# Gated blocks of two experts turned as one stack, down products two experts behind, in a one-core mixture-of-experts step

## What is computed

```python
def hier_moe(x, rg_w, rg_b, re_w, re_b, e_wg, e_wu, e_wd):
    pg = jax.nn.softmax((xt @ rg_w + rg_b).astype(f32), axis=-1)
    ...
    top_v, top_i = lax.top_k(pe, EXP_TOPK)
    ...
    for gi in range(N_GROUPS):
        h = jax.nn.silu(jnp.einsum('nd,edf->nef', xt, e_wg[gi])) * jnp.einsum('nd,edf->nef', xt, e_wu[gi])
        out = out + jnp.einsum('nef,efd->nd', h * comb[:, gi, :, None], e_wd[gi])
```

## Time and profile before

| what | value |
|---|---|
| time, median of 3 runs | 1253.25 us (1249.64 to 1254.41) |
| time of the profiled execution | 1249.23 us |
| its span in the profile | 1247.5 us |
| TensorE busy | 1219.0 us, 98% |
| VectorE, ScalarE busy | 593.5 us, 358.0 us |
| mean granted clock of TensorE | 0.993 |
| read from memory | 268.72 MB |

### The profile page before, as it was taken

How to read it: one execution, slowest core, us unless ns; L and a number is a source line. 1 busy time by engine, 2 the same in 40 slices (tenths; PEclk the granted TensorE clock), 3 DMA queues, 4 the chain that set the end, 5 groups by cost and what they waited for, 6 DMA issues and landing times.

```text
span 1247.5 us, 22834 instructions
## 1 busy us (share of the span) xinstructions
PE 1219.0 (98%) x9976; PEld 883.7 (71%) x9976; DVE 593.5 (48%) x942; ACT 358.0 (29%) x622; POOL 59.4 (5%) x99
## 2 busy tenths in 40 slices
PE   8999899999999999999999998999999999999997
PEld 8889888988898889999999885344444434444443
DVE  5346856544263543333334324445545545445545
ACT  6455343344224543322222321111111111111113
POOL 2100000001000100000000001000000000000000
PEclk9999999999999999999999999999999999999999
DMA  8210102302324723232223868999999999999993
GB/s 248 69 34 1 36 5 70 96 11 74 102 73 127 217 101 102 79 99 78 76 79 127 333 240 321 412 418 419 418 419 420 419 418 419 420 420 418 419 421 118
DMA packets 110206, 273.78 MB, mean 219 GB/s; under 512 B 22309, under 2 KB 69623, under 8 KB 85530
## 3 DMA queue, kind: packets, MB, share of 16 engines
q1 hardware_dynamic: 106234, 265.21, 56.1%
q0 software_dynamic: 2560, 4.73, 1.0%
q10 hardware_dynamic: 1312, 2.36, 0.5%
HBM read 268.72 MB, written 7.22 MB: 221 GB/s over the span
## 4 chain that ended last, share of the span: by engine, by line
PE 89%; DVE 8%; ACT 1%; issue 1%; DMA 0%; SPq 0%; ACTq 0%; DVEq 0%
PE bank L669 16%; PE bank L676 9%; PE bank L1523 7%; PE bank L817 7%; PE bank L1456 7%; PE bank L1458 7%; PE bank L1457 6%; PE bank L1583 2%; PE bank L1585 2%; PE bank L1584 2%; DVE yl L1106 2%; PE bank L864 2%; PE bank L1742 1%; PE bank L811 1%; PE bank L1696 1%
## 5 line engine op out<-in xcount | busy, mean ns | idle before, releaser
L669 PE MATMUL bank<-slot,xs 128*64 128x512 f32 x512 | 233.0, 599 | 0.9 <-DVE xs L1050 0.9
L670 PE MATMUL bank<-slot,xs 128*64 128x512 f32 x512 | 233.0, 599 | 0.0
L669 PEld LDWEIGHTS bank<-slot,xs 128*64 128x64 f32 x512 | 65.1, 137 | 124.6 <-issue 121.5
L1456 PE MATMUL bank<-xnh,wh 128*128 128x256 f32 (+1 forms) x448 | 133.3, 297 | 0.6 <-DVE mt L3087 0.6
L1458 PE MATMUL bank<-xnh,low 128*128 128x256 f32 (+1 forms) x448 | 132.8, 296 | 0.0
L1457 PE MATMUL bank<-xnl,wh 128*128 128x256 f32 (+1 forms) x448 | 132.8, 296 | 0.0
L1080 DVE TENSOR_TENSOR h<-h,bank 128x1024 f32<-128x1024 f32 (+1 forms) x73 | 86.4, 1215 | 88.9 <-PE bank L817 88.9
L2639 DVE TENSOR_TENSOR low<-ring,wh 128x1536 fp32r<-128x1536 f32 (+1 forms) x45 | 89.9, 2005 | 78.2 <-ACT wh L2278 71.3
L676 PE MATMUL bank<-slot,ht 128*64 128x512 f32 x512 | 116.9, 599 | 0.5 <-DVE ht L1100 0.5
L914 ACT ACTIVATE sg<-bank,csr 64x512 f32<-64x512 f32 x32 | 21.9, 684 | 270.4 <-PE bank L670 270.4
L1456 PEld LDWEIGHTS bank<-xnh,wh 128*128 128x128 f32 x448 | 85.1, 190 | 1.3 <-issue 1.2
(11 more groups left out here) (539 smaller groups left out, 2331.1 us busy)
## 6 DMA issues: line engine op xcount, KB each, us to landing
slot<-in_e_wg_dram SPq DMA_DIRECT2D x64, 1024.0 KB, 21.2
slot<-in_e_wu_dram SPq DMA_DIRECT2D x64, 1024.0 KB, 23.2
slot<-in_e_wd_dram SPq DMA_DIRECT2D x64, 1024.0 KB, 23.2
ring<-in_w_in_dram SPq DMA_DIRECT2D x13, 1024.0 KB, 5.3
ring<-in_w_in_dram SPq DMA_DIRECT2D x24, 512.0 KB, 4.2
ring<-in_w_branch_dram SPq DMA_DIRECT2D x24, 256.0 KB, 4.6
kvs<-in_cache_mem_k_dram SPq DMA_DIRECT2D x8, 512.0 KB, 5.8
kvs<-in_cache_mem_v_dram SPq DMA_DIRECT2D x8, 512.0 KB, 4.6
```

The lines of the kernel that those rows point to most:

```text
L669: pe.matmul(out[64:128, :], tok, wg[:, FF * k:FF * k + FF], start=(k == 0), stop=(k == KD - 1))
L670: mm = pe.matmul(out[0:64, :], tok, wu[:, FF * k:FF * k + FF], start=(k == 0), stop=(k == KD - 1))
L1456: pe.matmul(part, w_h, xh_(k, cols), start=(k == 0), stop=False)
```

## The change

Expert e's gated block now goes to the half of a 128-row tile that its parity names: even experts to rows 0 to 63, odd ones to rows 64 to 127, and the gate and up products swap their halves of bank 0 likewise. The block of a whole pair (two tiles `h2`, used in turn) is turned by 4 transposes of 128 rows (`turn_pair_h`), once in two experts, and one copy of 128 x 512 moves it to the one `ht`. As the pair is complete only after its odd expert, each down product stands two experts behind `gate_up`, and so do the down weights in the queue; expert 30 is followed by two down products, 31 by none. Mixing of pair i moves from beside expert 2i + 3 to beside expert 2i + 4, with its places after steps 3, 5 and 7; pair 14 stays beside expert 31. VectorE makes the fifth addition after the gated block. The diff, cut to its core:

```diff
-        sg = sb("sg", [CAP, FF], F32, z3 + 45056)
-        h2 = sb("h2", [CAP, FF], F32, z3 + 47104)
-        ht = [sb(f"ht{n}", [128, 4, CAP], F32, z3 + 49152 + 1024 * n) for n in range(2)]
+        sg = sb("sg", [128, FF], F32, z3 + 45056)
+        h2 = [sb(f"h2{n}", [128, FF], F32, at) for n, at in enumerate((z3 + 47104, z + 25088))]
+        ht = sb("ht", [128, 4, 2 * CAP], F32, z3 + 49152)
...
-            return HT_BANK if e == EX - 1 else 3
+            return HT_BANK if e in (EX - 3, EX - 1) else 3
+
+        def half_of(e):
+            return slice(CAP * (e % 2), CAP * (e % 2) + CAP)
+
+        def other_half(e):
+            return half_of(e + 1)
...
-        MIX_AFTER = {1: (0, 1), 4: (2, 3), 7: (4,)}
+
+        def mixed_beside(e):
+            if e == EX - 1:
+                return TWO - 2
+            return e // 2 - 2 if e >= 4 and e % 2 == 0 else None
+
+        MIX_AFTER = {3: (0, 1), 5: (2, 3), 7: (4,)}
...
+        def downs_behind(e):
+            return () if e < 2 or e == EX - 1 else (e - 2, e - 1) if e == EX - 2 else (e - 2,)
...
-            for e in range(3, EX + 1):
+            for e in range(3, EX + 2):
                 if e < EX:
                     for f in range(2):
                         pe_m.wait(sp, ("gu" if f else "gh", e - 3))
                         load(e, 0, (f,))
                         load(e, 1, (f,))
-                if e > 3:
-                    pe_m.wait(sp, ("d", e - 4))
-                    load(e - 1, 2)
+                if e > 4:
+                    pe_m.wait(sp, ("d", e - 5))
+                    load(e - 2, 2)
...
-                    if e >= 3 and e % 2:
+                    if mixed_beside(e) is not None:
                         for place in MIX_AFTER.get(k, ()):
-                            mix(e // 2 - 1, place)
+                            mix(mixed_beside(e), place)
...
             def down(e):
-                dve_e.wait(pe, ("ht", e))
-                if 1 <= e < EX - 1:
-                    dve_e.wait(pe, ("yl", e - 1))
+                dve_e.wait(pe, ("ht", e // 2))
+                if e >= 1 and e != EX - 3 and e != EX - 1:
+                    dve_e.wait(pe, ("yl", e - 2 if e == EX - 2 else e - 1))
...
-            def turn_h(e):
-                dve_e.wait(pe, ("h", e))
-                if e >= 1:
-                    dve_e.wait(pe, ("ht", e - 1))
+            def turn_pair_h(i):
+                dve_e.wait(pe, ("h", 2 * i + 1))
+                if i >= 1:
+                    dve_e.wait(pe, ("ht", i - 1))
+                if i == TWO - 1:
+                    dve_e.wait(pe, ("yl", EX - 3))
...
             for e in range(EX):
                 gate_up(e)
+                if e >= 2 and e % 2 == 0:
+                    turn_pair_h(e // 2 - 1)
                 if e + 1 < EX:
                     dve_e.wait(pe, ("xs", e))
                     turn_in(e + 1)
-                if e:
-                    down(e - 1)
-                turn_h(e)
+                for d in downs_behind(e):
+                    down(d)
+            turn_pair_h(TWO - 1)
+            down(EX - 2)
             down(EX - 1)
...
+            def turned_h(i):
+                pe_m.wait(dve, ("ht", i))
+                if i >= 1:
+                    pe_m.wait(dve, ("d", 2 * i - 1))
+                dve_e.done(dve.tensor_copy(ht[:, :, :], psum[HT_BANK][:, :].rearrange("p (f n) -> p f n", n=2 * CAP)), ("ht", i))
...
+            for e in range(EX):
+                if mixed_beside(e) is not None:
+                    for place in range(4):
+                        add(mixed_beside(e), place)
+                act_e.wait(dve, ("silu", e))
...
+                if e >= 2 and e % 2 == 0:
+                    turned_h(e // 2 - 1)
+                if mixed_beside(e) is not None:
+                    add(mixed_beside(e), 4)
                 if e + 1 < EX:
                     evacuate(e + 1)
...
+            turned_h(TWO - 1)
+            choose(TWO - 1)
+            low_rows(EX - 2)
+            low_rows(EX - 1)
```

More of the change, by code:

```diff
@@ L1084, in moe_dve @@
             act_t.wait(dve, "codes")
-            for e in range(EX + 1):
-                if e >= 3 and e % 2:
-                    for t in range(5):
-                        add(e // 2 - 1, t)
-                if e < EX:
-                    act_e.wait(dve, ("silu", e))
-                    if e >= 1:
-                        pe_m.wait(dve, ("ht", e - 1))
-                    dve_e.done(dve.scalar_tensor_tensor(h2[:, :], psum[0][0:64, :], csr[0:64, 1, e:e + 1], sg[:, :], ALU.mult, ALU.mult), ("h", e))
+            def turned_h(i):
[3 more added lines that the diff above has]
+                dve_e.done(dve.tensor_copy(ht[:, :, :], psum[HT_BANK][:, :].rearrange("p (f n) -> p f n", n=2 * CAP)), ("ht", i))
@@ new lines, in low_rows @@
+            def low_rows(d):
+                for r in range(2):
+                    act_e.wait(dve, ("yh", d, r))
+                    rows_ = slice(64 * r, 64 * r + 64)
+                    c = r ^ d % 2
+                    last = dve.scalar_tensor_tensor(yl[rows_, c, :], psum[y_bank(d)][rows_, :], csr[rows_, 0, d:d + 1], yh[rows_, c, :],
+                                                    ALU.mult, ALU.subtract)
+                dve_e.done(last, ("yl", d))
+            dve.wait_ge(far_stored, 16)
@@ new lines, in moe_dve @@
+            for e in range(EX):
+                if mixed_beside(e) is not None:
+                    for place in range(4):
+                        add(mixed_beside(e), place)
+                act_e.wait(dve, ("silu", e))
+                if e >= 4:
+                    pe_m.wait(dve, ("ht", e // 2 - 2))
+                dve_e.done(dve.scalar_tensor_tensor(h2[e // 2 % 2][half_of(e), :], psum[0][half_of(e), :], csr[half_of(e), 1, e:e + 1],
+                                                    sg[half_of(e), :], ALU.mult, ALU.mult), ("h", e))
+                if e >= 2 and e % 2 == 0:
+                    turned_h(e // 2 - 1)
+                if mixed_beside(e) is not None:
+                    add(mixed_beside(e), 4)
@@ L1109, in moe_dve @@
-                if e % 2:
-                    choose(e // 2)
+                if e >= 2 and e % 2 == 0:
+                    choose(e // 2 - 1)
+                for d in downs_behind(e):
+                    low_rows(d)
+            turned_h(TWO - 1)
+            choose(TWO - 1)
+            low_rows(EX - 2)
+            low_rows(EX - 1)
             dve.wait_ge(fg_loaded, 16)
```

91 lines of the change are left out of this document (42 added, 49 removed).

## The result

The changed kernel takes 1258.15 us in the median of 14 runs (1255.07 to 1267.04), the kernel before 1253.3 us in 14 runs beside it (1248.16 to 1256.27). The ratio, which goes by the means of these runs (1259.28 and 1252.31 us) and not by their medians, is 1.0056, with a 95% interval of 1.0036 to 1.0076: slower by a little over half a per cent. The forecast was 1259.9 us, and 1251 to 1263.5. The profiled execution has a span of 1253.6 us against 1247.5, so +6.1; forecast was 1254.1.

The account below looks back on a forecast made before the run. TensorE was taken to set the time, with the weight stream 1.7 us behind; span 1247.5 + 6.1 (end) + 0.5 (clock) = 1254.1, and median 1253.25 + 6.6 = 1259.9 us, range 1251 to 1263.5.

Parts of the forecast that it names:

- The reading of the two engines: Mixture of experts: TensorE takes 29.2 us a pair, the load stream 30.9; TensorE sets the time, stream 1.7 us behind.
- TensorE's saving: Expert pairs: one 128-row turn replaces two narrow ones; 7 us saved over 16 pairs if nothing else bound.
- a pair costs 28.7: TensorE's time per expert pair: 29.2 less 0.56 for the turn plus 0.1 of stall gives 28.7 us.
- The stall for the copy: Down product of an even iteration waits for the turned block's copy: 0.1 us a pair.
- The meeting with the stream: Before expert 30, all of TensorE's saving and 5.6 us more is waited away; `gate_up(30)` starts at 1187.4.
- The standstill at `down(29)`: TensorE waits 5.0 us for down weights 29, first half, landing at 1209.9; `down(29)` ends at 1214.3, ahead of expert 31.
- number 171: 1 MB half-load counted from expert 2's down weights; in the new order down weights 29, second half, landing at 1212.4.
- The end: After expert 31's gate product: `down(30)` starts at 1229.3, last down product ends at 1236.5, +6.1 us.
- The clock: TensorE's clock may halve after the 5.0 us standstill, costing 0 to 1.7 us; 0.5 added.
- case 2: Rival, load stream: it ends earlier as early gaps close; +3.9 us, 1257.2; chance 0.13.
- Case 3: Rival, load stream: not the wall, TensorE keeps its 7 us; -3 to -6 us, median 1248; chance 0.07.

Follow-up runs that it names:

- the run with the loads and the addition: Changed kernel, down weights 29 loaded ahead of expert 31's gate and up weights, VectorE's fifth addition behind the last copy; ratio 0.9993 to the kernel before.
- the kernel before with the swapped loads: Kernel before, with down weights 29 issued behind the gate and up weights of expert 31; ratio 1.0074 to the kernel before.
- the loads put right: Changed kernel, with down weights 29 issued ahead of the gate and up weights of expert 31; ratio 1.0022 to the kernel before.

## Why the prediction was right

**The reading of the two engines.** Right: TensorE and the stream were both full, and the stream was the slower by the pair. The two runs with a sixth fewer loads show it together. (The strip in the earlier trace rows stands at 9 from the 26th slice on, not the 25th.) In the changed kernel successive turns of stacked blocks stand 28.4 us apart as long as there is a lead, and further apart once TensorE has met the stream (the next one behind these stands at 1202.23, above):

```profile
1021.40 0.63 PE L884 MATMUL bank<-ident,h 128*128 128x128 f32 x4
...
1049.76 0.63 PE L884 MATMUL bank<-ident,h 128*128 128x128 f32 x4
...
1108.82 0.63 PE L884 MATMUL bank<-ident,h 128*128 128x128 f32 x4
...
1141.18 0.63 PE L884 MATMUL bank<-ident,h 128*128 128x128 f32 x4
...
1169.96 0.63 PE L884 MATMUL bank<-ident,h 128*128 128x128 f32 x4
```

The last three distances are 32.36, 28.78 and 32.27, in the mean 31.1, where I put the stream at 30.9; the two long ones weigh more in this mean than in a longer row. That long and short alternate I had not foreseen. In each long one are a wait of 2.0 to 2.2 us for a load and a fall of the clock, in the short one only a wait of 0.2. It is the falls that make the difference: in the run with the loads and the addition, without a fall, the same distances are 30.50, 30.58, 30.55 and 30.59.

**TensorE's saving.** Right in sign, mis-sized: the term "a pair costs 28.7" measured 28.4. The turn of 128 rows behind the mixing costs 0.46 (from 1202.23 to the turn of the input at 1202.69) where I took the 0.68 of `turn_in`, which saves 0.78 a pair, not 0.56. The stall for the copy is 0.30, not 0.1. These two cancel; the 0.4 that a pair is cheaper lies in steps that I had left as they were. A down product takes 3.48 where a gate product follows it, and 3.59 where the turn of the block followed, twice a pair:

```profile
1033.94 3.65 PE L694 MATMUL bank<-slot,ht 128*64 128x512 f32 x16
1037.42 0.59 PE L687 MATMUL bank<-slot,xs 128*64 128x512 f32 x1
```

`gate_up` with its mixing takes 12.34 (1037.42 to 1049.76) where I put 12.4, and the rest is in `gate_up` without mixing and in `turn_in`. For the first experts I had added 1 us; the waits for `xs` there are 4.1 us, where the kernel before waited 0.9 for `xs` and 1.0 for the gated block. It did not matter, as the stream swallowed all of it.

**The meeting with the stream.** The prediction says that all of TensorE's saving and 5.6 us more is waited away before expert 30. By its own sum the 5.6 us (1187.4 less 1181.8) are all that is waited there, less than the 6.7 us saved up to there (9.1 less 2.4), so the loss comes only behind it. Measured are 6.3 us of waits and two falls of the clock. `gate_up(30)` was forecast for 1187.4 and began at 1188.14: the load landed 0.6 later than I put it, and 0.1 lies between landing and start.

**The standstill at `down(29)`.** The step on which the forecast rests. Forecast were 5.0 us and 0.7; measured 3.21 and 0.45 (first half, second half). It was shorter because `down(28)` came 2.3 later (1203.64 for 1201.3), not because the load came earlier: number 171 landed at 1212.8, 0.4 later than I put it. The error of 2.3 us did not reach the end, because both halves of `down(29)` start when their loads land; a later `down(28)` only shortens the wait. Of the 2.3, 0.7 is the later start of `gate_up(30)`; from there to the first turn it took 14.1 us, 1.7 more than the forecast 12.4, which is the fall of the clock. The end of `down(29)` was forecast at 1214.3, and expert 31 began at 1214.66.

**The end.** `down(30)` was forecast for 1229.3 and began at 1229.60; the end was forecast for 1236.5 and came at 1236.61. That is +6.2 us at this point, forecast was 6.1. Within it I had the right distance from the gated block to `down(30)`, 2.0 us (1227.61 to 1229.60), but for the wrong terms: I laid 1.23 of it on the addition and left the turn out. Only 0.46 is the addition's, by the run with it moved; the turn and the copy take the rest.

**The clock.** The 0.5 us that I added were not used. The windows of the changed kernel:

```profile
1188.00:1192.00 4.00, 3.86 (x10) 0.57 1.01 420
...
1204.00:1214.00 10.00, 6.35 (x30) 1.00 1.01 421
...
1215.00:1230.00 15.00, 13.30 (x58) 1.00 0.33 138
```

The fall came in `gate_up(30)` (0.57 from 1188 to 1192), behind a wait of 2 us, and its 1.7 us came out of the standstill at `down(29)`. None followed in expert 31, although TensorE was busy for just 6.35 of the 10 us ahead of it. So the sum without the clock, 6.1, is what the span shows. That is in part luck. Behind the waits of 4.92 and 4.76 us ahead of the same down product, in the run with the addition moved and in the kernel before with the swapped loads, the clock did fall, and 1.7 and 1.9 us were lost. In both it had not fallen in `gate_up(30)`, so the standstill was longer than here.

The section HAM oscillation of the Trainium skill (TensorE: Matmul & The Clock Gate) let more be feared: there every wait for a transfer throttles. Those are waits of some 3 to 5 us, and to carry that over to the waits of 2 us was my step. Here two of the six waits for loads were followed by a fall, both of them of about 2 us, and that of 3.21 us was not. So falls do come behind the shorter waits, but not behind every wait.

**The rivals.** The stream did not end earlier (1222.8), so case 2 did not occur. Case 3 did not occur either: it came only with a sixth fewer loads, and then gave more than I put. The Trainium skill (DMA: Bandwidth & Descriptors, section Where 436 GB/s comes from) gives 435 GB/s as the ceiling of the fabric, and says that a load from memory is held lower, at about 358. The stream stood at 420 and 421 in the windows above, over 358 and below 435. The prediction says that at 435 case 3 would hold. By its own numbers it would not: 3.5% less than 30.9 us a pair is 29.8, still more than TensorE's 28.7.

**The time.** The forecast of +6.6 us stands between two readings of the result: the medians differ by 4.9 us, the means by 7.0. The span was met to 0.5 us, closer than the terms in it: the start of `down(28)` was 2.3 us off and the standstill 1.8, and the landings took up both.

What stays open is how often the clock falls in the standstill ahead of `down(29)`: it did in two of the three profiles with such a wait, and the median of the runs holds an unknown share of it.

## What to carry to other kernels

When one engine and a stream of loads are both full, measure the lead of each load over its use at the end of the loop, not the busy shares: it bounds what a faster engine can win (here the lead was 1.7 us, and TensorE alone had become faster by 9.1; the versions with the order mended won 0.2 to 1.8 of the stretch) and says from where on only the stream counts. There, a load that is waited for makes everything behind it late, so the order of the last loads must follow the order of their uses, with as little work as possible left behind each; work that a change moves to the end is paid in full. And check the order of the last iterations of a schedule by itself, since an irregular last step, as the two down products in a row here, asks for a load before its turn in the queue.

## What the runs showed of the hardware

- The spread between executions of one kernel is the clock: of the runs of the kernel before beside the one with the addition moved, the fastest took 1247.5 us at a mean granted clock of 0.994, the slowest 1256.8 at 0.986 (the line above is the same for all of them). A difference of 0.008 over 1250 us is some 20 us more at half clock, which loses 10. That is larger than the effect studied here, so profiles must be compared over the stretch in question.
- A wait for a load makes a fall of the clock possible and not sure. In the six profiles of the changed kernel and its versions with all loads and without small products, 19 waits of 1.8 to 2.2 us were followed by 5 falls of some 3.5 us at half clock: two of three in the changed kernel, two of two with the loads put right, one of three with the addition moved, none of eleven in the other three. Of the eight waits of 0.2 to 1.2 us none was followed by one. Behind 3.21 us it stayed up, behind 4.76 and 4.92 it fell.
- A fall that comes ahead of a load that is waited for anyway is free: the next wait shrinks from 2.0 to 0.2 or 0.3 us.
- What four transposes of 128 x 128 cost depends on their neighbours: 0.46 us from their start to that of the next group with the mixing ahead and transposes behind (1202.23 to 1202.69), and 0.68 with products of `gate_up` ahead and a down product behind (1204.51 to 1205.19). Which neighbour makes the difference no run shows.
